# Output weights of a hybrid decoder layer split second half first, in quarters, and the first expert weights issued behind the second branch product

## The chip, the cores and the metric

The kernel runs on one core of one Trainium2 chip. The metric is the device time of one execution in microseconds, and lower is better. Before the change the median of three runs is 793.13 us (791.08 to 793.21).

## The reference, cut to what matters

One decoder layer on a sequence of 512 tokens with a model width of 1024, all in float32. The mixer gives two branch outputs of width 512, one by gated linear attention and one by sparse attention. Each is projected to the model width, gated and added, and the sum goes through the output projection. A mixture of 32 experts follows.

```python
gates = jax.nn.sigmoid(bg.reshape(B, S, N_BRANCHES, D))
mix = gates[:, :, 0] * y_gla + gates[:, :, 1] * y_dsa
out = mix @ w_out[l]
x = x + gate_m * rmsnorm(out, g_post_mix[l])
h = rmsnorm(x, g_pre_ffn[l]) * (1.0 + scale_f) + shift_f
y = hier_moe(h, ...)      # top-1 of 4 groups, top-2 of 8 experts in it, gated MLPs
x = x + gate_f * rmsnorm(y, g_post_ffn[l])
```

## The kernel before, in words

Tokens lie in four tiles of 128 rows (`tt` = 0 to 3), and weights are taken in halves of 512 output columns (`n` = 0, 1). Most projections are done as split products: each float32 operand is written as a high part, rounded to `fp32r`, and a low part, the rest. TensorE then multiplies high by high, high by low and low by high (`split_matmul`, L480 to L482). The high part is a cast on ScalarE (`split_hi`, L1313, semaphore `hi_ready`). The low part is a subtraction on VectorE (`split_lo`, L1794, semaphore `lo_ready`), and it waits for the high part. Both take a whole weight (128x4096 elements) or one quarter of it (128x1024). `split_at` gives each weight its place in the order in which these two semaphores are counted, so whoever waits for a weight also waits for all that stand ahead of it in `split_order`.

The large on-chip `arena` is cut into areas 0 to 3, "H" and "B", and "G" is the tile `gvs`. The two halves of the output weights, `("out", 0)` and `("out", 1)`, live in "H" with their high part in "B", and in "G" with their high part in area 1.

Transfers are issued from SyncE's queue (SP) in a written order. `items` numbers the weights, and `ring_out` counts the products that are done with theirs. Item 18, `("out", 1)`, is loaded once `ring_out` is 15. Item 17, `("out", 0)`, waits for 16, the end of the last input projection, since "H" and "B" hold the split activations until then. Behind item 17, SP issues `first_gate_up(0)`: 2 MB of the first expert's gate and up weights in rows of 1 KB, into area 0. It then waits for `ring_out` 17 (`("proj", 1)` + 1, the end of the second branch product) and issues `first_gate_up(1)` and two down weights of 1 MB each. The next group (`gate_up(1, ...)`, 4 MB) waits for 18, which TensorE signals inside `out_half(2, 1)`, and the one behind it for 19.

TensorE does, in this order, the last input projection, `branches(1, tt)` for four token tiles, `router_bias`, `mix_turn(0)` and `mix_turn(1)` (transposes of the mixed rows), and then the eight `out_half` products. `branches(n, tt)` makes two results of 12 matmuls each in the PSUM banks A0 and A1 by turns. `split_wait(("out", n))` at the head of `out_half` waits for both parts of that weight.

VectorE frees the banks A0 and A1. Per token tile, `mixing(n, tt)` multiplies both results by their gates (L2036) and adds them (L2040). The table `after` says which low parts VectorE works off between two calls of `mixing`. Behind the last `mixing` come `mix_copy(0)`, one more low part and `mix_copy(1)` (L2113). `residual(tt)` (L2078) needs rows of the input `x`, whose transfer ScalarE issues on its own queue (L1585).

On ScalarE, the high parts of both output halves come behind the last `sigmoid`, half 0 first, each as one cast and each behind the wait for its load.

Of the kernel before, what the change touches and what calls it, by code (L numbers as in the profile page):

```python
# [25 lines left out]
D = 1024  # L26
# [55 lines left out]
def layer(nc, x, c, positions, w_ada, b_ada, g_pre_mix, g_post_mix, g_pre_ffn, g_post_ffn, w_in,  # L82
# [17 lines left out]
    with ExitStack() as ctx:  # L100
# [10 lines left out]
        def sem(name):  # L111
            return ctx.enter_context(nc.semaphore(name))
# [123 lines left out]
        ada_spot = (0, 1, "H", "B")  # L236

        split_order = [("in", O_DK), ("in", O_DQ), ("in", O_DV), ("in", O_GQ), ("in", O_GV), ("in", O_GG), ("in", O_BG), ("in", O_BG + D),
                       ("proj", 0), ("in", O_BG + 512), ("in", O_BG + D + 512), ("proj", 1), ("out", 0), ("out", 1)]
        home = {key: ((0, 1), (3, 2))[n % 2] for n, key in enumerate(split_order)}  # L240
        home[("out", 0)], home[("out", 1)] = ("H", "B"), ("G", 1)
        area["G"], area_r["G"] = gvs[:, :], gvs_r[:, :]
# [67 lines left out]
        ring_out = sem("ring_out")  # L310
# [57 lines left out]
        item_at = {it: n for n, it in enumerate(items)}  # L368
# [6 lines left out]
        def ring_wait(eng, it):  # L375
            n = item_at[it]

            extra = sum(1 for m, o in enumerate(items[:n + 1]) if m % 4 == n % 4 and o[0] == "proj")
            eng.wait_ge(ring_in[n % 4], 16 * (n // 4 + 1 + extra))
# [9 lines left out]
        def _(pe):  # L389
# [567 lines left out]
            def other_part(tt):  # L957

                pe.wait_ge(fss_ready, tt + 1)
                for half, (name, _) in enumerate(sum_banks[tt]):  # L960
                    last = nc.tensor.matmul(ps[name][:, :], ident[:, :], yc[:, tt, 0, 512 * half:512 * (half + 1)], start=False, stop=True)
                last.then_inc(sum_full, 1)
# [11 lines left out]
        def _(sp):  # L974
# [59 lines left out]
            def first_gate_up(q):  # L1034
                for n, src in enumerate((w_e_gate, w_e_up)):
                    dst = gu_sets[0][q][:, 2048 * n:2048 * (n + 1)].rearrange("p (k f) -> p k f", k=KD)
                    sp.dma_start(dst, src[0][q].rearrange("(k p) f -> p k f", p=P)).then_inc(we_in[0], 16)
# [10 lines left out]
            def next_down(z, e0, e1_, turn):  # L1048

                sp.wait_ge(bank["A1"].full, moe_base["A1"] + turn)  # L1050
                down(z, 0, e0)
                down(z, 1, e1_)
# [4 lines left out]
            def pair_down(j):  # L1057
                next_down(j % 3, 2 * j, 2 * j + 1, j - 2)

            first_gate_up(0)  # L1060
            sp.wait_ge(ring_out, item_at[("proj", 1)] + 1)
            first_gate_up(1)
            down(0, 0, 0)
            down(0, 1, 1)
# [209 lines left out]
        def _(act):  # L1274
# [34 lines left out]
            def split_hi(key, q=None):  # L1309

                src, _, hi = splits[key]
                part = slice(None) if q is None else slice(1024 * q, 1024 * (q + 1))
                nc.scalar.copy(hi[:, part], src[:, part]).then_inc(hi_ready, 4 if q is None else 1)  # L1313
# [132 lines left out]
            for u in range(NU + 1):  # L1446
                tq, hp = u // PAIRS, u % PAIRS
                n = (tq + 1) * P
# [66 lines left out]
                for tt in range(1, TT):  # L1515
                    sigmoid(1, ab, tt)
            act.wait_ge(ring_out, item_at[("in", O_BG + D + 512)] + 1)
            for n in range(2):
                ring_wait(act, ("out", n))
                split_hi(("out", n))  # L1520

            def out_squares(tt, n):

# [162 lines left out]
            def square(tt):  # L1686

                if tt == 0:
                    act.wait_ge(sum_ready, 1)
                    nc.scalar.activation(scratch2, yc[:, tt, 0, :], ACT.Square, accum_out=st[:, tt:tt + 1]).then_inc(fms_ready, 1)  # L1690
                    return
                act.wait_ge(sum_full, tt + 1)
                for half, (name, _) in enumerate(sum_banks[tt]):
                    n = tt + 20 * half
                    nc.scalar.activation(scratch2[:, 512 * half:512 * (half + 1)], ps[name][:, :], ACT.Square, accum_out=st[:, n:n + 1]).then_inc(fms_ready, 1)
# [19 lines left out]
        def _(dve):  # L1715
# [73 lines left out]
            def split_lo(key, q=None):  # L1789

                src, lo, hi = splits[key]
                part = slice(None) if q is None else slice(1024 * q, 1024 * (q + 1))
                dve.wait_ge(hi_ready, split_at[key] + (4 if q is None else q + 1))
                V.tensor_tensor(lo[:, part], src[:, part], hi[:, part], ALU.subtract).then_inc(lo_ready, 4 if q is None else 1)  # L1794
# [236 lines left out]
            def mixing(n, tt):  # L2031

                for ab in range(2):
                    dve.wait_ge(sig_ready, n * 2 * TT + ab * TT + tt + 1)
                    a, free = filled(dve, ("y", n, tt, ab))
                    step(V.tensor_tensor(sig[:, ab, tt, :], a[:, :], sig[:, ab, tt, :], ALU.mult))  # L2036
                    dve.sem_inc(free, 1)  # L2037
                if n == 0 and tt == 0:
                    filled(dve, ("att", TT * PAIRS - 1), "O")
                V.tensor_tensor(mix[:, tt, n * 512:(n + 1) * 512], sig[:, 0, tt, :], sig[:, 1, tt, :], ALU.add).then_inc(mix_ready, 1)  # L2040
# [3 lines left out]
            split_lo("q")  # L2044
            split_lo(("proj", 0))
            bg0, bg1 = ("in", O_BG + 512), ("in", O_BG + D + 512)
            after = {(0, 1): [(bg0, 0), (bg0, 1)], (0, 2): [(bg0, 2), (bg0, 3)], (0, 3): [(bg1, None)], (1, 0): [(("out", 0), 0), (("out", 0), 1)],
                     (1, 1): [(("out", 0), 2), (("out", 0), 3)], (1, 2): [(("out", 1), 0), (("out", 1), 1), (("out", 1), 2)]}
            for n in range(2):
                for tt in range(TT):  # L2050
                    mixing(n, tt)
                    for key, q in after.get((n, tt), ()):
                        split_lo(key, q)
                if n == 0:
                    split_lo(("proj", 1))
            dve.wait_ge(mix_ready, 2 * TT)

            def shifted(dst, src, k, done, scale, shift):
# [47 lines left out]
            def mix_copy(tt):  # L2106

                if tt >= 2:
                    filled(dve, ("out", tt - 2, 1))
                for half in range(2):  # L2110
                    t, free = filled(dve, ("mix", tt, half))
                    dve.wait_ge(mixT_ready[0], 2 * tt + half + 1)
                    V.tensor_tensor(mixT(tt % 2, 1, 512 * half, 512), t[:, :], mixT(tt % 2, 0, 512 * half, 512), ALU.subtract).then_inc(mixT_ready[1], 1)  # L2113
                    dve.wait_ge(mixT_ready[1], 2 * tt + half + 1)
                    dve.sem_inc(free, 1)
# [39 lines left out]
            dve.sem_inc(free, 1)  # L2155
            step(V.tensor_tensor(w_rt[:, :, :], w_rt[:, :, :], scale_n.unsqueeze(2).broadcast_to([P, KD, GROUPS + NE]), ALU.mult))
            mix_copy(0)
            split_lo(("out", 1), 3)
            mix_copy(1)
            out_scaled(0, 0)  # L2160
            out_scaled(0, 1)
# [180 lines left out]
            def add_last(tt):  # L2342

                dve.wait_ge(fss_ready, tt + 1)
                dve.wait_ge(sum_full, tt + 1)
                for half, (name, _) in enumerate(sum_banks[tt]):
                    y = yc[:, tt, 0, 512 * half:512 * (half + 1)]
                    step(V.tensor_tensor(y, ps[name][:, :], y, ALU.add))
                dve.sem_inc(sum_ready, 1)

            def scaled(tt):

                if tt == 0:
                    step(V.tensor_tensor(yc[:, tt, 1, :], yc[:, tt, 0, :], gfb, ALU.mult))
                else:
                    for half, (name, _) in enumerate(sum_banks[tt]):
                        part = slice(512 * half, 512 * (half + 1))
                        step(V.tensor_tensor(yc[:, tt, 1, part], ps[name][:, :], gfb[:, part], ALU.mult))
# [55 lines left out]
```

## Time and profile before

| | us |
|---|---|
| median of three runs | 793.13 |
| lowest and highest run | 791.08 and 793.21 |
| profiled execution: its span, first to last instruction | 789.2 |
| median less that span, the part outside the first and last instruction, as far as it can be told | 3.9 |
| TensorE busy | 703.0 (89%) |
| VectorE busy | 411.7 (52%) |
| ScalarE busy | 287.7 (36%) |

The trace gives no total of its own for the profiled execution beside the span, so the span and the 3.9 us around it stand for it. Times within the span are counted from its first instruction.

In the page, each digit of a row of 40 is the busy share of one slice of 19.7 us. In a timeline, a row is the start, the duration (the sum, where several instructions follow each other), the engine, the line, the operation, the tiles written and read, their shapes and the count. In square brackets stands how long the engine was idle before it, and what ended that.

### The profile page before, as it was taken

The page shows a single profiled execution, that of the slowest core. Times are in us where ns is not written, and L with a number is a line of the kernel's source. Part 1 is how long each engine was busy: PE and PEld are TensorE (multiplying, and loading weights), DVE is VectorE, ACT ScalarE, POOL GpSimd, SP SyncE. Part 2 cuts the span into 40 slices and gives each one's busy share as a digit, 9 for nine tenths or more (in the row PEclk, how much of TensorE's full clock was granted, in tenths as well). Part 3 has the DMA queues.
Part 4 walks back from the last instruction along what each step waited for, and adds up shares of the span by engine and source line. Part 5 has one row for each costly group of instructions (what it writes and reads, how often), then busy time and mean ns, then how long its engine had stood idle before and what let it go on. Part 6 is the DMA issues. An engine that isn't in the chain of part 4 may idle for free.

```text
span 789.2 us, 9728 instructions
## 1 busy us (share of the span) xinstructions
PE 703.0 (89%) x3451; PEld 447.0 (57%) x3451; DVE 411.7 (52%) x876; ACT 287.7 (36%) x514; POOL 120.9 (15%) x148
## 2 busy tenths in 40 slices
PE   1799989998998999999999899989979978878784
PEld 0347747666776777777787678873423323323221
DVE  2386858998897665654422636572533211112118
ACT  5233255254447768642022315344112211112223
POOL 3064852210002022000000000101121221111100
PEclk9999989999999889999999999999989998989997
DMA  9989730411302030023334472599999999999982
GB/s 337 396 311 364 283 142 1 116 44 64 107 9 99 1 107 1 5 104 107 107 123 161 142 267 79 229 374 391 418 422 418 420 419 419 421 420 413 409 327 108
DMA packets 50300, 179.27 MB, mean 227 GB/s; under 512 B 9624, under 2 KB 13826, under 8 KB 36428
## 3 DMA queue, kind: packets, MB, share of 16 engines
q1 hardware_dynamic: 44308, 166.26, 54.1%
q0 software_dynamic: 4784, 8.19, 2.9%
q10 hardware_dynamic: 1160, 4.20, 1.4%
q8 instruction: 28, 0.46, 0.2%
q14 instruction: 20, 0.16, 0.1%
HBM read 174.13 MB, written 12.59 MB: 237 GB/s over the span
## 4 chain that ended last, share of the span: by engine, by line
PE 48%; SPq 13%; DVE 13%; DMA 8%; ACT 4%; issue 3%; POOL 0%; DVEq 0%; ACTq 0%; POOLq 0%; PEldq 0%
PE psA L480 10%; PE psA L482 10%; PE psA L481 10%; SPq L1032 5%; SPq L1090 4%; SPq L1040 4%; PE psS L884 3%; PE psA L913 3%; DMA arena<-in_w_e_up_dram 2%; PE psG L884 2%; DVE mk_mem L1846 2%; DMA y_dram<-sig_mem,tables 2%; DVE m L1845 2%; PE psO L611 1%; PE psT L598 1%
## 5 line engine op out<-in xcount | busy, mean ns | idle before, releaser
L480 PE MATMUL psA<-arena_r 128*128 128x512 f32 x320 | 130.8, 409 | 3.5 <-DVE arena_r L1794 2.9
L481 PE MATMUL psA<-arena_r 128*128 128x512 f32 x320 | 127.0, 397 | 0.0
L482 PE MATMUL psA<-arena_r 128*128 128x512 f32 x320 | 126.8, 396 | 0.0
L1794 DVE TENSOR_TENSOR arena_r<-arena,arena_r 128x1024 fp32r<-128x1024 f32 (+1 forms) x37 | 60.4, 1654 | 38.4 <-ACT arena_r L1313 37.4
L480 PEld LDWEIGHTS psA<-arena_r 128*128 128x128 f32 x320 | 61.5, 192 | 24.4 <-issue 12.3
L482 PEld LDWEIGHTS psA<-arena_r 128*128 128x128 f32 x320 | 61.5, 192 | 13.5
L481 PEld LDWEIGHTS psA<-arena_r 128*128 128x128 f32 x320 | 61.5, 192 | 12.2 <-issue 0.2
L884 PE MATMUL psG<-arena,kv 128*64 128x512 f32 x208 | 61.2, 642 | 7.6 <-issue 7.6
L884 PE MATMUL psS<-arena,kv 128*64 128x512 f32 x224 | 58.5, 611 | 9.8 <-issue 7.9
L1313 ACT CAST arena_r<-arena 128x1024 fp32r<-128x1024 f32 (+1 forms) x31 | 49.9, 1630 | 20.6 <-DMA arena<-in_w_in_dram 10.2
L913 PE MATMUL psA<-qs_mem,sig_mem 128*64 128x512 f32 x80 | 39.5, 637 | 4.4 <-ACT sig_mem L1637 4.4
L2291 DVE TENSOR_TENSOR sig_mem<-sig_mem,psS 128x256 f32<-128x256 f32 x8 | 4.9, 613 | 72.7 <-ACT sig_mem L1632 72.7
L1239 POOL DMA_INDIRECT y_dram<-sig_mem,tables x16 | 15.9, 994 | 174.6 <-issue 108.5
L480 PE MATMUL psA<-arena_r,qs_mem_r 128*128 128x512 f32 x96 | 38.1, 397 | 4.2 <-DVEq L2037 3.3
L2291 DVE TENSOR_TENSOR sig_mem<-sig_mem,psG 128x256 f32<-128x256 f32 x8 | 4.9, 612 | 70.7 <-ACT sig_mem L1632 70.7
L884 PEld LDWEIGHTS psS<-arena,kv 128*64 128x64 f32 x224 | 20.1, 140 | 37.4 <-issue 36.9
L884 PEld LDWEIGHTS psG<-arena,kv 128*64 128x64 f32 x208 | 19.6, 147 | 33.5 <-issue 32.8
L472 PE MATMUL psA<-arena,kv 128*128 128x512 f32 x64 | 29.2, 619 | 2.3 <-DMA arena<-in_w_in_dram 2.3
L481 PE MATMUL psA<-arena_r,qs_mem_r 128*128 128x512 f32 x80 | 31.1, 389 | 0.0
L1646 ACT COPY sig_mem<-psA 128x512 f32<-128x512 f32 x16 | 9.4, 586 | 55.7 <-PE psA L913 32.2
L1411 ACT ACTIVATE sig_mem<-psA 128x512 f32<-128x512 f32 x16 | 9.6, 598 | 50.8 <-PE psA L482 50.8
L1845 DVE MAX8 m<-mk_mem 128x8 f32<-128x256 f32 (+2 forms) x48 | 26.9, 560 | 2.2
(443 smaller groups left out, 1304.2 us busy)
## 6 DMA issues: line engine op xcount, KB each, us to landing
arena<-in_w_e_gate_dram SPq DMA_DIRECT2D x24, 1024.0 KB, 17.0
arena<-in_w_e_up_dram SPq DMA_DIRECT2D x24, 1024.0 KB, 19.4
arena<-in_w_in_dram SPq DMA_DIRECT2D x11, 2048.0 KB, 8.8
arena<-in_w_e_down_dram SPq DMA_DIRECT2D x12, 1024.0 KB, 18.6
qs_mem<-in_w_e_down_dram SPq DMA_DIRECT2D x10, 1024.0 KB, 23.0
arena<-in_w_ada_dram SPq DMA_DIRECT2D x4, 2048.0 KB, 16.8
qT<-in_w_ada_dram SPq DMA_DIRECT2D x6, 1024.0 KB, 5.4
gvs<-in_w_ada_dram SPq DMA_DIRECT2D x5, 1024.0 KB, 6.3
```

The costliest lines, as they stand in the source:

```text
L472: last = nc.tensor.matmul(a[:, :], hT[:, k, tt * P:(tt + 1) * P], w[:, k, :], start=(k == 0), stop=(k == KD - 1))
L480: nc.tensor.matmul(acc, lhs[0], rhs[0], start=start, stop=False)
L481: nc.tensor.matmul(acc, lhs[0], rhs[1], start=False, stop=False)
L482: return nc.tensor.matmul(acc, lhs[1], rhs[0], start=False, stop=stop)
L884: last = nc.tensor.matmul(ps[g][64 * q:64 * q + 64, :].rearrange("p (g f) -> p g f", g=2), h2g[:, b, k, 64 * q:64 * q + 64], gu, start=(k ...
L913: last = nc.tensor.matmul(ps[name][64 * q:64 * q + 64, :], actT[:, b, kf, 64 * q:64 * q + 64], down_sets[z][q][:, D * kf + 512 * n:D * kf ...
L1032: sp.dma_start(dst, src[bass.ds(e, 1), :, :].rearrange("a p n -> p (a n)")).then_inc(we_in[z], 16)
L1040: sp.dma_start(down_sets[z][q], wed_v[bass.ds(e, 1), :, :].rearrange("a p n -> p (a n)")).then_inc(wd_in[z], 16)
L1090: sp.dma_start(gu_sets[z][q][:, 2048 * n:2048 * (n + 1)][:, part], src[2 * j + q][:, part]).then_inc(we_last[j - (NPAIR - 2)] if half else ...
L1313: nc.scalar.copy(hi[:, part], src[:, part]).then_inc(hi_ready, 4 if q is None else 1)
L1794: V.tensor_tensor(lo[:, part], src[:, part], hi[:, part], ALU.subtract).then_inc(lo_ready, 4 if q is None else 1)
L1845: step(V.max(m8[:, :], work))
```

## The change

The two halves of the output weights change places in `split_order`. ScalarE casts half 1 first and does both in quarters. VectorE's low parts are dealt out anew: one quarter of half 1 comes before the first second-half `mixing`, and none is left between `mix_copy(0)` and `mix_copy(1)`. SP issues `first_gate_up(0)` behind the wait for `ring_out` 17 and no longer ahead of it.

```diff
-                       ("proj", 0), ("in", O_BG + 512), ("in", O_BG + D + 512), ("proj", 1), ("out", 0), ("out", 1)]
+                       ("proj", 0), ("in", O_BG + 512), ("in", O_BG + D + 512), ("proj", 1), ("out", 1), ("out", 0)]
...
+            sp.wait_ge(ring_out, item_at[("proj", 1)] + 1)
             first_gate_up(0)
-            sp.wait_ge(ring_out, item_at[("proj", 1)] + 1)
             first_gate_up(1)
...
             act.wait_ge(ring_out, item_at[("in", O_BG + D + 512)] + 1)
-            for n in range(2):
+            for n in (1, 0):
                 ring_wait(act, ("out", n))
-                split_hi(("out", n))
+                for q in range(4):
+                    split_hi(("out", n), q)
...
-            after = {(0, 1): [(bg0, 0), (bg0, 1)], (0, 2): [(bg0, 2), (bg0, 3)], (0, 3): [(bg1, None)], (1, 0): [(("out", 0), 0), (("out", 0), 1)],
-                     (1, 1): [(("out", 0), 2), (("out", 0), 3)], (1, 2): [(("out", 1), 0), (("out", 1), 1), (("out", 1), 2)]}
+            after = {(0, 1): [(bg0, 0), (bg0, 1)], (0, 2): [(bg0, 2), (bg0, 3)], (0, 3): [(bg1, None)], (1, 0): [(("out", 1), 1), (("out", 1), 2)],
+                     (1, 1): [(("out", 1), 3), (("out", 0), 0), (("out", 0), 1)], (1, 2): [(("out", 0), 2), (("out", 0), 3)]}
...
                 if n == 0:
                     split_lo(("proj", 1))
+                    split_lo(("out", 1), 0)
...
             mix_copy(0)
-            split_lo(("out", 1), 3)
             mix_copy(1)
```

## Rows read from the trace of the kernel before

**Rows 1.** The page: TensorE's total, DMA share and GB/s of 40 slices

```profile
PE 703.0 (89%) x3451; PEld 447.0 (57%) x3451; DVE 411.7 (52%) x876; ACT 287.7 (36%) x514; POOL 120.9 (15%) x148
...
DMA  9989730411302030023334472599999999999982
GB/s 337 396 311 364 283 142 1 116 44 64 107 9 99 1 107 1 5 104 107 107 123 161 142 267 79 229 374 391 418 422 418 420 419 419 421 420 413 409 327 108
```

**Rows 2.** The chain of waits, 395 to 540 us: start, us, what

```profile
428.73 7.84 DMA arena<-in_w_out_dram
436.67 3.64 ACT arena_r L1313
...
443.50 0.47 PE psA L480
...
461.02 0.43 PE psA L480
...
472.65 0.87 PE psS L726 x8
```

**Rows 3.** Timeline of ScalarE around the casts of the output weights

```profile
428.71 0.60 ACT L1411 ACTIVATE sig_mem<-psA 128x512 f32<-128x512 f32 x1 [4.84 <-PE psA L482]
436.67 3.63 ACT L1313 CAST arena_r<-arena 128x4096 fp32r<-128x4096 f32 x1 [7.37 <-DMA arena<-in_w_out_dram]
```

**Rows 4.** All casts of line 1313: ns least, median, most

```profile
L1313 ACT CAST arena_r<-arena x31: 1031/1050/3635, 42.1 to 436.7; 128x1024 fp32r<-128x1024 f32 x24, 128x4096 fp32r<-128x4096 f32 x7
```

**Rows 5.** Timeline of TensorE, 425 to 470 us

```profile
439.76 0.39 PE L482 MATMUL psA<-arena_r,qT_r 128*128 128x512 f32 x1
443.50 0.47 PE L480 MATMUL psA<-arena_r,qs_mem_r 128*128 128x512 f32 x1 [3.35 <-DVEq L2037]
...
449.06 0.39 PE L480 MATMUL psA<-arena_r,qs_mem_r 128*128 128x512 f32 x1
...
454.28 0.39 PE L482 MATMUL psA<-arena_r,qT_r 128*128 128x512 f32 x1
454.97 1.95 PE L745 MATMUL psG<-w_rt,gla_mem 128*128 128x36 f32 x16 [0.30 <-PE psA L482]
...
459.08 1.94 PE L726 MATMUL psS<-ident,kv 128*128 128x128 f32 x8 [1.27 <-DVEq L2115]
```

**Rows 6.** Timeline of VectorE, 430 to 476 us

```profile
432.10 0.69 DVE L2036 TENSOR_TENSOR sig_mem<-psA,sig_mem 128x512 f32<-128x512 f32 x1 [9.75 <-PE psA L482]
434.82 0.69 DVE L2036 TENSOR_TENSOR sig_mem<-psA,sig_mem 128x512 f32<-128x512 f32 x1 [2.03 <-PE psA L482]
435.66 0.69 DVE L2040 TENSOR_TENSOR kv<-sig_mem 128x512 f32<-128x512 f32 x1
440.33 2.36 DVE L1794 TENSOR_TENSOR arena_r<-arena,arena_r 128x1024 fp32r<-128x1024 f32 x2 [3.98 <-ACT arena_r L1313]
442.61 0.68 DVE L2036 TENSOR_TENSOR sig_mem<-psA,sig_mem 128x512 f32<-128x512 f32 x1
...
450.78 3.49 DVE L1794 TENSOR_TENSOR gvs_r<-gvs,arena_r 128x1024 fp32r<-128x1024 f32 x3
454.19 0.68 DVE L2036 TENSOR_TENSOR sig_mem<-psA,sig_mem 128x512 f32<-128x512 f32 x1
...
475.70 1.42 DVE L2078 SCALAR_TENSOR_TENSOR gqk<-gqk,st,qs_mem 128x512 f32<-128x512 f32 x2
```

**Rows 7.** Timeline of SP's queue: transfers of output and expert weights

```profile
407.37 0.51 SPq L1000 DMA_DIRECT2D gvs<-in_w_out_dram  x1
...
454.79 0.37 SPq L1037 DMA_DIRECT2D arena<-in_w_e_gate_dram  x1
...
501.91 0.33 SPq L1032 DMA_DIRECT2D arena<-in_w_e_gate_dram  x1
```

**Rows 8.** Windows: us, PE, PEld, DVE, ACT, POOL busy (count), PEclk, DMA share, GB/s

```profile
440.20:443.50 3.30, 0.00 (x1) 0.03 (x1) 2.96 (x3) 3.30 (x2) 0.00 (x0) 1.00 0.55 173
454.80:470.50 15.70, 14.27 (x72) 12.22 (x73) 6.70 (x11) 2.93 (x6) 0.00 (x0) 0.89 0.91 333
459.00:462.00 3.00, 2.92 (x11) 2.62 (x12) 2.54 (x4) 1.17 (x2) 0.00 (x0) 0.50 1.10 363
472.00:498.00 26.00, 26.00 (x149) 22.37 (x148) 14.59 (x43) 14.35 (x25) 3.71 (x2) 1.00 0.17 62
506.00:736.00 230.00, 203.80 (x1016) 88.93 (x1014) 70.36 (x202) 55.13 (x125) 30.46 (x30) 0.96 1.01 412
```

**Rows 9.** Transfer queues from 466 to 467 us: packets, MB, share of 16 engines

```profile
q1 hardware_dynamic: 34, 0.28, 66.8%
q10 hardware_dynamic: 33, 0.14, 33.7%
```

**Rows 10.** Transfers of `x` rows issued at line 1585, and one at line 1537

```profile
L1585 ACTq DMA_DIRECT2D qs_mem<-in_x_dram x2: 388/414/440, 461.1 to 461.5; - x2
...
DMA to landing us min/median/max: 8.2/9.3/10.5
...
qs_mem<-in_x_dram ACTq DMA_DIRECT2D x1, 512.0 KB, 3.1
```

## The prediction

> **What bounds the kernel now.** I read the page first. TensorE is busy for 89% of the span, but the last third tells another story: from slice 27 to 38 the DMA row is at 9 and the rate near 420 GB/s [rows 1]. A window confirms it: from 506 to 736 us the share is 1.01 at 412 GB/s, while TensorE has 26 us idle in these 230 [rows 8]. The expert stage is a stream of weights that runs back to back once it is released. The release is SP's issue at 501.91 us, which waits for a product inside the output projection [rows 7]. So what counts is how early that point comes.
>
> The chain of waits leads back from there. From 461 us to the release it is TensorE at work with no gap. Ahead of it stands one detour: the load of half 0 of the output weights (428.73, 7.84 us), its cast (436.67, 3.64 us), and only at 443.50 a matmul again [rows 2]. The timelines show how a load for a later product stops this one. ScalarE is free after its sigmoid at 429.3 us, but its first cast waits 7.37 us for that load [rows 3]. VectorE is done with the first `mixing` at 436.3 us and stands at the low part of half 0 for 3.98 us. After two low parts it gets to the next gate multiplication at 442.61 [rows 6]. TensorE holds both PSUM banks full meanwhile: its last matmul starts at 439.76, the next at 443.50, 3.35 us idle [rows 5].
>
> **The casts and low parts: the wait goes, a small one comes.** Matmuls here start every 0.227 us (449.06 to 454.28 us is 23 steps, 5.22 us) [rows 5]. Without a wait the matmul of 443.50 would start at 439.76 + 0.23 = 439.99.
>
> Half 1 was issued at 407.37 us [rows 7], over 20 us before `ring_out` reached 16. Its first quarter is cast at 429.3 to 430.35 (1.05 us, the median of that form) and the fourth is done by 433.5 [rows 3, 4]. Its first low part (1.18 us, half of 2.36) ends at 431.6. It stands ahead of the `mixing` that started at 432.10 after 9.75 us idle [rows 6], so it costs nothing; its cover is 0.5 us, and a cast later by more than that would push the mixing one for one. The quarters of half 0 follow the landing, 436.6 us, and end by 440.9. Four quarters cost 4 x 1.05 = 4.2 us against 3.63 for the whole [rows 4]; the next work of ScalarE is over 10 us later, so 0.6 us is hidden.
>
> VectorE, by the distances of its rows [rows 6]: two low parts of half 1 from 436.3, then the gate multiplication at 438.5, which ends at 439.2. A bank comes free 0.89 us after such a start (442.61 to 443.50 [rows 5, 6]), at 439.4, so TensorE goes on at 439.99. The second result is complete at 440.15; multiplication at 440.26, addition at 441.1. Now come three low parts, where before there were two. Three of them and the next multiplication are 3.41 us apart (450.78 to 454.19 [rows 6]): 441.7 + 3.41 = 445.1. The bank is free at 446.0. TensorE wants it at 439.99 + 24 x 0.227 = 445.43. That is what is late next, **0.57 us**, a wait that was not there.
>
> The matmul of 449.06 us thus starts at 446.0, 3.06 us sooner. A restart costs about 0.1 us (the first step is 0.30 and not 0.227), in both kernels, once at another place. The last matmul of the branch products moves from 454.28 to about 451.3, **3.0 us** sooner. The two low parts left (447.5 to 449.9) fall under TensorE's work. All eight are there by 449.9, so the wait of `out_half` for both halves costs nothing: that product starts near 461.0 - 3.0 = 458.0 [rows 2]. The cover is 8 us.
>
> The low part taken out between `mix_copy(0)` and `mix_copy(1)` (1.2 us) stands behind the bank release that TensorE waits for at 459.08 [rows 5], and ahead of rows needed a product later. I count it at 0; its bounds are 0 and 0.2 us.
>
> **The moved transfers.** SP issued the first 2 MB right behind half 0. Now they stand behind `ring_out` 17, 454.79 - 3.0 = 451.8 us, with the other 4 MB. Queued behind them on SP is the group that waits for 18, near 498.9, and nothing else. Moved are six transfers, 6.29 MB, and 1.05 MB of `x` rows from ScalarE: 7.34 MB. At the 333 GB/s of the same stretch [rows 8] they end at 451.8 + 22.0 = 473.8 us. From there to the release the chip moves little now (share 0.17 from 472 to 498 [rows 8]), so the cost to the stream is 0. Without that idle stretch 2.1 MB at 412 GB/s would cost 5.1 us. The experts first need the weights after 530 us.
>
> The `x` rows are the near miss. They were issued at 461.1, landed 8.2 and 10.5 us later [rows 10] and were first needed at 475.70 [rows 6]. Now they are issued near 458.1 and needed at 472.7, with some 2.1 MB more ahead. If the transfers share the engines as before, the first tile lands at 466.3: cost 0. If it has to stand behind the extra 2.1 MB as well (5.8 us at 363 GB/s), it lands at 472.1: still 0, by 0.6 us. What speaks for sharing: from 466 to 467 us ScalarE's queue (q10) moved 33 packets and SP's (q1) 34 [rows 9]. The Trainium skill (DMA: Bandwidth & Descriptors, section on queues, rings and completion order) says that each engine goes round between the queues packet by packet; by that rule, the trace agrees, the first landing applies.
>
> **Sum.** 3.51 us of wait gone, less 0.57 of new wait: 3.0 rounded. The expert stream, its releases and the tail keep their distances. The profiled execution has a span of 789.2 and gets 786.2; the median lies 3.9 us over that span, and the same 3.9 gives 790.1. As the runs spread over 2.1 us, this stall may have been longer or shorter in others; it ends with the landing of one load.
>
> **Rivals.**
> A. The clock stretch goes. The clock granted to TensorE is 1.00 through the idle 440.2 to 443.5, but 0.50 (1.2 GHz) from 459 to 462 [rows 8]. There eight transposes take 1.94 us [rows 5] and 0.87 us later on, and three to four matmul steps 0.43 instead of 0.23 [rows 2]: 1.07 + 0.7 = 1.8 us. With other timing ahead it may be spared: 788.3. The Trainium skill (TensorE: Matmul & The Clock Gate, part 1) says that the chip's measure runs free of the program, so an equal gap can fall either way.
> B. The reverse: one more such stretch, beside the new small wait or ahead of the output products: 790.1 + 1.8 = 791.9. For it: the gap at 459 was only 1.27 us. Against: the long gap at 440 did not do it.
> C. It does nothing: the expert stage takes its pace from elsewhere, or half 0 lands so late that VectorE still waits. 793.1. Against: the engine row is full from 506 us, and half 0 is cast 5 us before it is wanted (437.7 against 442.9).
> D. Slower: the `x` rows are served only after all SP transfers. 6.29 MB at 333 GB/s end at 470.7, and a tile alone takes 3.1 us [rows 10]: 473.8. `residual(0)` then comes 1.1 us late, and TensorE's transposes, which follow it, by some 0.6: 790.7. It decides against the kernel only if the rows of 1 KB run slower. At 280 GB/s the tile lands at 477.4, and the time is 794.3; the change loses from 476.2 on, about 295 GB/s. Against: 363 GB/s from 459 to 462 us, in these very rows [rows 8].
>
> **How the numbers follow.** Forecast 0.60 (own range 789.0 to 791.4: the new wait between 0 and 1.5 us, and a stall of another length), A 0.10, B 0.11, C 0.08, D 0.11, of it 0.04 near 790.7 and 0.07 at 793 and above. The range 788.0 to 793.0 takes in A, B and the mild end of D, and leaves out most of C and the rest of D, about 0.15 to 0.2. No change is within 0.3%, 2.4 us, about what a measurement of this kernel can tell. The forecast clears it by 0.6 us only, so a fifth of its chance falls within. Faster: 0.48 of the forecast and 0.10 of A, 0.58. Within: 0.12 of the forecast, B, C and the mild D, 0.35. Slower: 0.07.
>
> **What would show it.** Casts of half 1 from 429 us in quarters; no idle TensorE at 440, and about 0.6 us near 445.5; last branch matmul at 451.3; SP's group of six at 451.8; the release at 498.9; all later marks 3 us sooner. A first `x` tile landing after 472.7, or clock 0.50 elsewhere between 440 and 500, would make the number wrong, and so would a stream whose end does not follow its release.

## The result and the profile after

| | before | changed |
|---|---|---|
| median of 13 runs, us | 791.41 (788.33 to 796.73) | 785.11 (783.77 to 790.76) |
| ratio, changed to before | | 0.9942, 95% interval 0.9922 to 0.9963 |
| span of the profiled execution, us | 789.2 | 789.0 |

The change makes the kernel 4.6 us faster by the ratio (2.9 to 6.2 us), and 6.3 us by the medians. The forecast was 3.0 us faster, 790.1 us in a range of 788.0 to 793.0, so the direction was right, and the time lies below the range. The interval of this ratio takes in the forecast's 3.0 us, so it does not show by itself that the gain is larger. In the experiments below two single executions took 2402.74 us (the kernel before) and 3903.55 us (both gaps filled), which the ratios leave out.

The two profiled executions hide this. The changed one took 790.76 us, the slowest of its 13 runs, and its span equals that of before. The profile's page shows the same work in it:

```profile
PE 704.7 (89%) x3451; PEld 448.5 (57%) x3451; DVE 411.9 (52%) x876; ACT 289.0 (37%) x520; POOL 120.6 (15%) x148
...
DMA  9989740402303030033324293699999999999972
```

So the stage has to be read by itself. On ScalarE, half 1 is cast in quarters right behind the last sigmoid, and half 0 from its landing on (timeline of ScalarE, changed kernel):

```profile
431.48 3.91 ACT L1313 CAST arena_r<-gvs 128x1024 fp32r<-128x1024 f32 x4 [0.17 <-ACT sig_mem L1411]
438.72 3.91 ACT L1313 CAST arena_r<-arena 128x1024 fp32r<-128x1024 f32 x4 [3.34 <-DMA arena<-in_w_out_dram]
```

VectorE, same kernel. The 3.98 us ahead of the low parts of half 0 [rows 6] are gone, and the first low part is done 0.38 us before the first mixing can start:

```profile
432.56 1.23 DVE L1795 TENSOR_TENSOR gvs_r<-gvs,arena_r 128x1024 fp32r<-128x1024 f32 x1 [8.05 <-ACT arena_r L1313]
434.17 0.69 DVE L2037 TENSOR_TENSOR sig_mem<-psA,sig_mem 128x512 f32<-128x512 f32 x1 [0.38 <-PE psA L482]
...
444.91 2.35 DVE L1795 TENSOR_TENSOR arena_r<-arena,arena_r 128x1024 fp32r<-128x1024 f32 x2
447.18 0.69 DVE L2037 TENSOR_TENSOR sig_mem<-psA,sig_mem 128x512 f32<-128x512 f32 x1
```

TensorE, same kernel: its rows with an idle time, and the one ahead of the new wait. In place of 3.35 us idle [rows 5] there is one wait of 0.41 us, behind the three low parts in a row. Counted as the prediction counts, from where the next matmul would have started (447.27 + 0.23), it is 0.57 us:

```profile
431.05 0.47 PE L480 MATMUL psA<-arena_r,qs_mem_r 128*128 128x512 f32 x1 [0.44 <-PE psA L482]
...
447.27 0.39 PE L482 MATMUL psA<-arena_r,qT_r 128*128 128x512 f32 x1
448.07 0.47 PE L480 MATMUL psA<-arena_r,qs_mem_r 128*128 128x512 f32 x1 [0.41 <-DVEq L2038]
...
454.05 1.95 PE L745 MATMUL psG<-w_rt,gla_mem 128*128 128x36 f32 x16 [0.30 <-PE psA L482]
...
458.17 1.94 PE L726 MATMUL psS<-ident,kv 128*128 128x128 f32 x8 [1.27 <-DVEq L2117]
```

From the first matmul of the second branch product to the router bias it takes 454.05 - 431.05 = 23.00 us. Before it took 454.97 - 429.02 = 25.95 us; the first matmul of the kernel before is

```profile
429.02 0.47 PE L480 MATMUL psA<-arena_r,qs_mem_r 128*128 128x512 f32 x1 [0.41 <-PE psA L482]
```

That is 2.95 us less. But this execution came to the stage 2.03 us later, and it had 0.86 us more behind the first expert product.

SP's queue and the windows of the changed kernel (us, PE, PEld, DVE, ACT, POOL busy, PEclk, DMA share, GB/s):

```profile
453.87 0.37 SPq L1037 DMA_DIRECT2D arena<-in_w_e_gate_dram  x1
...
500.86 0.33 SPq L1032 DMA_DIRECT2D arena<-in_w_e_gate_dram  x1
```

```profile
453.87:473.00 19.13, 17.68 (x91) 15.11 (x92) 5.96 (x12) 3.72 (x9) 0.00 (x0) 0.91 0.99 340
457.00:462.00 5.00, 3.83 (x15) 3.31 (x16) 2.77 (x4) 1.81 (x4) 0.00 (x0) 0.66 1.10 359
...
505.00:735.00 230.00, 203.17 (x1011) 89.19 (x1011) 70.30 (x202) 55.31 (x125) 30.32 (x30) 0.96 1.01 412
```

The six transfers move through an otherwise idle stretch, and the expert stream keeps its share of 1.01 and 412 GB/s [rows 8]. The clock at the first transposes fell in this execution too. The `x` rows, moved earlier with the rest, landed faster than before [rows 10]:

```profile
L1586 ACTq DMA_DIRECT2D qs_mem<-in_x_dram x2: 388/414/439, 460.2 to 460.6; - x2
...
DMA to landing us min/median/max: 7.1/7.8/8.4
```

### The profile page after: what moved, and what is told of

Its sections match the earlier page's. It is cut to its first block, busy times and chain, and to the rows that moved or that the text cites. A ratio compares the mean times of both kernels' runs of the same rounds, so it can differ in the third digit from the quotient of the medians.

```text
span 789.0 us, 9733 instructions
## 1 busy us (share of the span) xinstructions
PE 704.7 (89%) x3451; PEld 448.5 (57%) x3451; DVE 411.9 (52%) x876; ACT 289.0 (37%) x520; POOL 120.6 (15%) x148
## 4 chain that ended last, share of the span: by engine, by line
PE 56%; DVE 13%; DMA 7%; SPq 5%; issue 5%; ACT 3%; POOL 0%; DVEq 0%; ACTq 0%; POOLq 0%
PE psA L480 11%; PE psA L482 10%; PE psA L481 10%; PE psS L884 5%; PE psA L913 5%; SPq L1090 4%; PE psG L884 4%; DMA arena<-in_w_e_up_dram 2%; DVE mk_mem L1847 2%; DMA y_dram<-sig_mem,tables 2%; DVE m L1846 2%; PE psO L611 1%; PE psT L598 1%; PE psS L588 1%; DMA xn_dram<-sig_mem 1%
```

## The experiments

Two questions: which edit gives the 2.95 us, and where the rest of the 4.6 us comes from. The expectations name three theories: the wait alone counts (1), the wait and falls of TensorE's clock count (2), the moved transfers matter (3). "The stage" is the stretch from the first matmul of the second branch product to the router bias, and a "fall" is a stretch in which the granted clock is 0.50. All ratios are to the kernel before, run beside each kernel.

**The two kernels again, and the change in two parts.** The first kernel is the one before and the second the changed one, both unedited.

> The kernel before, unchanged, under a name of its own, to see how far two sets of executions of one kernel lie apart on this chip and what granted clock each has. Theory 1 (the stall alone): the branch-product stretch from the first matmul of the second branch product to the router bias is 25.9 us as in the trace before, and the time is equal to before within 0.2%. Theory 2 (stall plus clock): the idle 3.35 us at 440 us also lets TensorE's clock fall to half in some executions, so the executions fall into groups 2 to 5 us apart, and the slower group has the lower mean clock. Theory 3 (the moved transfers matter): says nothing on this one.

> The changed kernel, unchanged, beside the others of this job. Theory 1: 3.0 us (0.38%) under before, the rest of the 4.6 us (ratio 0.9942) being chance in when the executions were taken. Theory 2: 4 to 6 us under before, with a mean clock higher by 0.003 to 0.006. The branch-product stretch is 23.0 us in its trace under either.

The SP edit alone:

```diff
-            first_gate_up(0)
             sp.wait_ge(ring_out, item_at[("proj", 1)] + 1)
+            first_gate_up(0)
             first_gate_up(1)
```

> Only the SP edit: the first expert's 2 MB behind the wait for the second branch product, nothing else changed. Theory 1 and 2: the stall at 440 us stays 3.3 us, give or take 0.5, the time is that of before within 0.2%. Theory 3: the load of half 0 lands sooner without 2 MB behind it (under 7 us instead of 7.84), the stall shrinks by as much, and the time falls by 1 to 2 us.

All but the SP edit:

```diff
-            sp.wait_ge(ring_out, item_at[("proj", 1)] + 1)
             first_gate_up(0)
+            sp.wait_ge(ring_out, item_at[("proj", 1)] + 1)
             first_gate_up(1)
```

> All of the change but the SP edit: half 1 first, quarters, low parts dealt out anew, the first expert's 2 MB issued early as before. Theory 1: the stall is gone, the time is that of the changed kernel within 0.1%, 3 us under before. Theory 2: the same, 4 to 6 us under before. Theory 3: between before and the changed kernel, at least 1 us over the changed one.

| | median, us | ratio, 95% interval |
|---|---|---|
| before again | 789.20 | 0.9979 (0.9954 to 1.0004) |
| changed again | 784.70 | 0.9926 (0.9887 to 0.9964) |
| SP edit alone | 789.56 | 0.9985 (0.9959 to 1.0012) |
| all but the SP edit | 785.29 | 0.9940 (0.9913 to 0.9968) |

The unedited kernel lies 0.2% from itself, so differences of that size are not told apart here. Its twelve executions (786.35 to 792.21 us) do not part into the groups that theory 2 asked for. The SP edit does nothing that can be seen, and the split order with its quarters does all that can be seen. The load of half 0 is not helped by having no 2 MB behind it: with the SP edit alone it lands in 7.8 us (the least of the two output loads; 7.84 before [rows 2]), and ScalarE's wait for it (7.4 us) and VectorE's behind that (3.97 us) are as before (output weights' transfers, and timeline of VectorE).

```profile
  ACT arena_r L1313: 7.4, 1
...
DMA to landing us min/median/max: 7.8/10.1/12.4
```

```profile
441.72 2.36 DVE L1794 TENSOR_TENSOR arena_r<-arena,arena_r 128x1024 fp32r<-128x1024 f32 x2 [3.97 <-ACT arena_r L1313]
```

Theory 3 falls by this wait; the time alone would not rule out its 1 to 2 us. The trace of the kernel before, taken again, shows what that of the prediction did not. Its matmuls behind the wait start every 0.43 us and not every 0.23 us, at a granted clock of 0.57 in the window (timeline of TensorE and a window):

```profile
440.73 0.70 PE L480 MATMUL psA<-arena_r,qs_mem_r 128*128 128x512 f32 x1 [3.48 <-DVEq L2037]
441.23 0.63 PE L481 MATMUL psA<-arena_r,qs_mem_r 128*128 128x512 f32 x1
441.65 0.63 PE L482 MATMUL psA<-arena_r,gqk_r 128*128 128x512 f32 x1
```

```profile
440.50:444.50 4.00, 3.77 (x10) 2.99 (x11) 3.64 (x5) 0.53 (x1) 0.00 (x0) 0.57 0.00 0
```

The stage took 27.68 us in this execution instead of 25.95: 1.7 us for one fall. And in the changed kernel's second trace the clock stays full at the first transposes, where it fell in the first one:

```profile
451.00:460.00 9.00, 7.55 (x42) 6.19 (x42) 3.42 (x6) 2.25 (x4) 0.00 (x0) 1.00 1.07 356
```

**The wait in another size.** The kernel before, with the casts in quarters only:

```diff
                 ring_wait(act, ("out", n))
-                split_hi(("out", n))
+                for q in range(4):
+                    split_hi(("out", n), q)
```

> The kernel before with one edit: the high parts of both halves cast in quarters, half 0 still first. The first low part can start about 1.0 us after the load and not 3.6 us after it, so TensorE's wait at 440 us should shrink from 3.5 to about 1.0 us. Theory 1 (the wait alone): 2.4 to 2.6 us under before. Theory 2 (wait plus clock): 3.5 to 4.5 us under before, as a short wait no longer lets the clock fall, and no stretch at 0.50 between 438 and 446 us in the trace. A third possibility, that only a load out of the way helps: no gain.

788.12 us, ratio 0.9968 (0.9944 to 0.9991). The wait is 0.87 us:

```profile
436.98 0.47 PE L480 MATMUL psA<-arena_r,qs_mem_r 128*128 128x512 f32 x1 [0.87 <-DVEq L2038]
```

The stage took 23.50 us, 2.45 less than before, and the ratio gives 2.5 us. That was theory 1's number. Theory 2 was right that no fall comes near 440. Its 3.5 to 4.5 us did not appear, though the interval (0.7 to 4.4 us) does not rule them out, and the trace has a fall at 514 to 518 us instead. Most of the stage's gain was to be had with these two lines.

**Work in the gaps.** `filler` writes products nobody reads into a free bank. The kernel before with the wait filled:

```diff
             for tt in range(TT):
+                if tt == 2:
+                    filler("S1", 12)      # 12 matmuls of 512 columns
                 branches(1, tt)
```

> The kernel before with 12 extra matmuls (2.7 us) into an unused bank at the place of the wait at 440 us, so that TensorE is at work in nearly all of the wait, which itself stays. The extra products are thrown away. Theory 1: the same time as before within 0.1%. Theory 2: 0.8 to 1.8 us under before, the share of executions in which the clock fell there times its price of about 1.7 us. If the filler delays the product behind it, up to 0.3 us more.

788.25 us, ratio 0.9975 (0.9951 to 0.9999): 2.0 us, just above theory 2's 0.8 to 1.8. There was no fall at 440, while the stage (26.36 us) was not shorter than in the trace of the prediction, which had no fall there either. The interval nearly reaches 1, and the kernel against itself gave 0.9979, so this alone shows little.

The changed kernel with the second gap filled:

```diff
             mix_turn(0)
+            split_wait(("out", 1))
+            filler("O", 5)
             mix_turn(1)
```

> The changed kernel with 5 extra matmuls (1.1 us) into an unused bank between the two first transposes of mixed rows, where TensorE idles 1.27 us. Their results are thrown away. Theory 2 and rival A of the prediction (the half-clock stretch at 457 to 462 us hangs on this gap): the stretch goes in all executions, 1 us gained on the mean over the changed kernel, router bias to first output product 5.35 us and not 5.71. Theory 1: the same time as the changed kernel within 0.1%, or 0.2 us more.

783.73 us, ratio 0.9922 (0.9899 to 0.9945), with the clock full:

```profile
451.00:460.00 9.00, 8.71 (x46) 6.95 (x45) 3.42 (x6) 2.25 (x4) 0.00 (x0) 1.00 1.08 360
```

The full clock stood there without the filler in three of four traces of this product order, all three of executions that came early to the stage, as this one did (see the table below). So the gain over the changed kernel (0.2% by ratio) is not shown.

Both gaps filled in the kernel before, by the two edits together, with half 0 as the second filler's operand:

> The kernel before with extra matmuls in both gaps: 12 in the wait at 440 us and 5 between the two first transposes of mixed rows. Their results are thrown away. Theory 1: the time of before within 0.1%. Theory 2: 2 to 3 us under before; what then stays to the changed kernel with the second gap filled alike is the bare wait, 2.9 us.

789.34 us (788.73 without the one long execution), ratio 0.9990 (0.9970 to 1.0010): a miss for theory 2. The trace has no fall at 440 or at the transposes, but one at 528 to 532 us, and the stretch to the first expert product is 110.6 us, longer than in the trace of the prediction (109.8). With both gaps filled a fall still came, only later.

**The wait put back.** The changed kernel, with TensorE waiting at the old place for something VectorE finishes about 3 us later:

```diff
             for tt in range(TT):
+                if tt == 2:
+                    pe.wait_ge(lo_ready, split_at[("out", 1)] + 4)
                 branches(1, tt)
```

> The changed kernel, with an idle wait put back at the old place: TensorE waits ahead of the third token tile of the second branch product for the last low part of half 1, about 3.0 us idle, while the 0.4 us wait one tile later falls away. Casts, low parts and transfers stay as changed. Theory 1 (the wait alone counts): 2.6 us over the changed kernel. Theory 2 (wait plus clock): 3.5 to 4.5 us over it, so within 1 us of before, and the granted clock falls to 0.50 behind the wait or at the first transposes in more of the executions.

The same with `filler("S1", 11)` ahead of the wait:

> The kernel of the run ahead with 11 extra matmuls (2.5 us) into an unused bank inside the wait. Their results are thrown away. The wait's end is the same, TensorE is only not idle in it. Theory 1: the time of the run ahead within 0.1%. Theory 2: 1 to 1.7 us under it, and 2.6 us over the changed kernel.

Idle: 789.73 us, ratio 0.9985 (0.9967 to 1.0002), the kernel before again. Filled: 787.41 us, ratio 0.9968 (0.9946 to 0.9989). Windows of the two at the wait:

```profile
441.00:446.00 5.00, 4.96 (x15) 3.96 (x16) 2.50 (x3) 0.00 (x0) 0.00 (x0) 0.66 0.00 0
```

```profile
441.00:446.00 5.00, 4.67 (x21) 3.55 (x20) 4.48 (x5) 0.16 (x1) 0.00 (x0) 1.00 0.00 0
```

The idle wait costs 3.4 us over the changed kernel by the ratios (0.9985 against 0.9942), the filled one 2.1 us, with 2.4 us more in the stage. The order is that of theory 2, with sizes just under its 3.5 to 4.5 and 2.6. But the intervals of the two overlap, and theory 1's 2.6 us for both lies within both, so the times do not decide.

**The delay as work, in two sizes.** The changed kernel with 13, then 7, extra matmuls at that place, with no wait:

```diff
+                if tt == 2:
+                    filler("S1", 13)      # and 7
```

> The changed kernel with 13 extra matmuls (2.95 us) into an unused bank ahead of the third token tile of the second branch product: the old delay back, but as work and with no idle at all. Their results are thrown away. Theory 2a (the idle wait lets the clock fall): 2.6 us over the changed kernel (the 0.4 us wait one tile later falls away), with no fall at 440 us. Theory 2b (the delay itself moves the later gaps to where the clock falls): 3.5 to 4.5 us over it, with a fall between 455 and 530 us.

> The same with 7 extra matmuls (1.59 us). Theory 2a: 1.2 us over the changed kernel. Theory 2b: anything from 1.2 to 3 us over it, by where the gaps then come to lie; a fall between 455 and 530 us in the trace if it is over 2.

13: 785.98 us, ratio 0.9949 (0.9930 to 0.9968), the stage 2.26 us longer, no fall from 435 to 530 us. 7: 786.48 us, ratio 0.9959 (0.9935 to 0.9983), the stage 1.07 us longer, a fall at 520 to 524 us. The larger delay does not bring the loss back (0.6 us by ratio, even under theory 2a's 2.6), so theory 2b does not hold as put. Its interval is some 1.5 us wide on each side, as is that of the changed kernel, so theory 2a's 2.6 is not ruled out. The trace of the smaller one has a fall without any whole idle wait ahead of it, so theory 2a is not all either. That of the larger one is of an execution that came late to the stage, that of the smaller one of an early one, so the two are not quite alike.

**One more trace of each, and the version from it.**

> The kernel before, one more trace. Both theories below need the count of executions in which the granted clock falls between 435 and 545 us. If a fall belongs to the kernel with the wait, there is at least one here, as in the two traces of it so far, and the stretch from the first matmul of the second branch product to the first expert product takes 109.8 us or more.

> The changed kernel, one more trace. If the falls went with the wait, there is none between 435 and 545 us and the stretch takes 105.6 us, as in one of the two traces of it so far; the other had one fall and 106.7 us.

The trace of before had falls at 439 to 444 and 456 to 461 us, the changed one none from 435 to 530. The small new wait is taken out by one low part moved on:

```diff
-(1, 1): [(("out", 1), 3), (("out", 0), 0), (("out", 0), 1)], (1, 2): [(("out", 0), 2), (("out", 0), 3)]}
+(1, 1): [(("out", 1), 3), (("out", 0), 0)], (1, 2): [(("out", 0), 1), (("out", 0), 2), (("out", 0), 3)]}
```

> The changed kernel with one low part moved on: two and not three behind the second mixing, three behind the third. The wait at 448 us (0.4 us, predicted as 0.57) should be gone, first matmul to router bias 22.6 us and not 23.0. Theory 1 and 2 alike: 0.4 us under the changed kernel, which the time alone can hardly tell; if the third mixing then holds up the transposes, no gain or 0.3 us lost.

783.22 us, ratio 0.9918 (0.9893 to 0.9943). The stage took 22.35 us, 0.65 less than changed: the 0.57 us of the wait and its restart. With the filler between the transposes as well:

> The best version so far: the changed kernel with two and not three low parts behind the second mixing, and 5 extra matmuls between the first two transposes. Their results are thrown away. Both theories: 0.4 us under the kernel with the extra matmuls alone, some 7 us under before (ratio 0.991), if the two edits add up; the same as either if the first one brought nothing.

782.76 us over six executions, ratio 0.9906 (0.9880 to 0.9932), the fastest kernel here, ahead of both. Its interval overlaps that of the one ahead of it and that of the changed kernel.

## Where the 4.6 us come from

The table sets marks side by side in all traces, in us, from the timelines of TensorE and SP. The marks are the first matmul of the second branch product (its time stands in the first column), the router bias (L745), the first output product, and SP's first issue behind the first expert product. The last column says where the granted clock was under 1 from 435 to 530 us.

| kernel | first matmul at | first matmul to bias | bias to output product | first matmul to expert product | clock fell near |
|---|---|---|---|---|---|
| before, of the prediction | 429.0 | 25.95 | 5.71 | 109.8 | 459 |
| before again | 426.1 | 27.68 | 5.71 | 111.6 | 440, 457 |
| before, one more | 425.3 | 27.77 | 5.71 | 111.6 | 439, 456 |
| SP edit alone | 430.4 | 26.04 | 5.71 | 109.9 | 460 |
| changed | 431.1 | 23.00 | 5.71 | 106.7 | 457 |
| changed again | 426.3 | 22.96 | 5.35 | 105.6 | none |
| changed, one more | 427.2 | 23.17 | 5.34 | 105.9 | none |
| all but the SP edit | 426.1 | 22.96 | 5.35 | 105.6 | none |
| quarters only | 424.9 | 23.50 | 5.34 | 107.7 | 514 |
| before, wait filled | 430.7 | 26.36 | 5.71 | 110.1 | 460 |
| before, both filled | 429.9 | 26.29 | 5.34 | 110.6 | 528 |
| changed, idle wait back | 427.1 | 27.04 | 5.34 | 111.3 | 441, 520 |
| changed, wait filled | 429.5 | 25.44 | 5.35 | 109.7 | 521 |
| changed, 13 extra | 429.7 | 25.26 | 5.34 | 107.9 | none |
| changed, 7 extra | 424.6 | 24.07 | 5.34 | 108.4 | 520 |
| changed, transposes filled | 426.0 | 22.97 | 5.34 | 105.7 | none |
| changed, low part moved | 426.6 | 22.35 | 5.34 | 105.0 | none |
| both of these | 425.2 | 22.32 | 5.35 | 105.0 | none |

The first four have TensorE's order of before, the next four that of the change. Their means over the whole stretch are 110.7 and 106.0 us, a difference of 4.7 us, and the ratio says 4.6. It has three parts:
- The wait: 2.95 us, in every pair without a fall at it.
- A fall at the wait: 1.7 us, in two of the four traces of before and none of the changed. Of all traces it comes in three of the five with the whole wait idle, and in none of the 13 others. That gives 0.9 us on the mean.
- A fall at the first transposes: 0.36 us to the output product, and 0.8 us within it and its followers up to the release (40.4 against 41.2 us), 1.15 us in all. It comes in four of four before and one of four changed, which gives 0.9 us on the mean.

A fall near 514 to 528 us, in five of the other traces, takes 1.5 to 1.6 us between the release and the first expert product (38.5 against 36.9 us).

That 4.7 meets 4.6 so closely is luck, as each mean rests on four traces and the ratio's interval is 2.9 to 6.2 us. That the gain is over 3.0 us is better founded: the 33 executions of the changed order in the first two measurements have a mean of 785.9 us, the 68 of the order of before, SP edit alone counted in, 790.4, which is 4.6 us, by their scatter 3.6 to 5.6 (an estimate; it pools two measurements).

**The falls go with the arrival.** The first column parts the traces into two groups that the list above mixes. In seven the first matmul comes late, at 429.0 to 431.1 us, in eleven early, at 424.6 to 427.2. That is settled ahead of anything that differs between these kernels: from 268 to 284 us the granted clock was 0.68 or less in each of the seven, and 1.00 in each of the eleven (windows of before, then of before again):

```profile
268.00:284.00 16.00, 15.64 (x83) 11.64 (x84) 6.98 (x21) 7.90 (x20) 4.03 (x5) 0.68 0.00 2
```

```profile
268.00:284.00 16.00, 15.25 (x116) 11.54 (x116) 10.30 (x28) 10.12 (x22) 4.04 (x5) 1.00 0.01 2
```

Five traces have the whole wait idle. The clock fell behind it in the three early ones (before again, before one more, idle wait back) and in neither of the two late ones (before, SP edit alone). The length of the idle time does not sort them: 2.83, 3.48 and 3.51 us were followed by a fall, 3.33 and 3.35 us were not. At the transposes the order of before has a fall in both groups, and the changed order only in the one late trace of its four (two late traces with a delay put into it had none there). So over the stretch to the first expert product the change takes 3.1 us off a late execution (109.8 and 109.9 to 106.7) and 5.9 us off an early one (111.6 twice to 105.6, 105.9 and 105.6). The 4.6 us is a mix of the two, and how often each comes was not measured. These two prices rest on few traces, one changed one for the late group.

## Why the prediction was wrong, step by step

**Casts and low parts: right.** No wait was left at the third tile. The new one at the fourth came as 0.41 us idle, which by the prediction's own count is its 0.57 us. The stage lost 2.95 us for a forecast of 3.0. The 0.5 us of cover for the first low part was 0.38 us.

**The moved transfers: right.** The group was issued 22.8 us behind the first matmul, as worked out (451.8 against 429.0). The `x` rows landed 7.1 us after their issue, so rival D is out, and the SP edit alone changes nothing that can be seen. Rival C is out as well: the expert stream follows its release, 249.5 to 251.3 us from the first expert product to the end in all traces but one (253.5).

**The sum: this is the step that failed.** "The expert stream, its releases and the tail keep their distances", and before that 3.51 less 0.57, took the clock of one execution as a fixed part of the kernel and put what the clock would change at nothing. The rows showed a long idle wait without a fall, and the argument read that as a property of the wait. In executions that come early to the stage the same wait costs 1.7 us more, and the fall at the transposes, kept in the sum on both sides, is gone with the change in them. On the mean of the traces these two terms make some 1.7 us. Rival A had the last one, at 1.8 us for a measured 1.15, and gave it a chance of 0.10, where three of four traces show it. It counted the eight transposes at 0.87 us without a fall; they take 1.47 us from first start to last end, with 0.19 us of waiting for VectorE among them (changed again):

```profile
453.36 0.63 PE L726 MATMUL psS<-ident,kv 128*128 128x128 f32 x4 [1.26 <-DVEq L2117]
454.17 0.66 PE L726 MATMUL psS<-ident,kv 128*128 128x128 f32 x4 [0.19 <-DVEq L2117]
```

Rival B's argument "the long gap at 440 did not do it" rested on one trace, of a late execution, and the next trace refutes it.

**The step to the median** was off by 1.7 us as well. It put 3.9 us around the span, where every profiled execution since shows about 1.8 us between span and time (790.76 against 789.0). By that the profiled execution of before was the one of 791.08 us: near the later median of 791.41 over 13 executions, and 2 us under the 793.13 of the first three.

Either of the two alone would have left 788.4 us, inside the range. Together they give 786.7, and by the ratio 786.8. The median of 785.11 lies 1.7 us lower still. Eight of the 13 changed executions took 783.8 to 786.0 us at a mean granted clock of 0.963 to 0.968, and four took 788.4 to 790.8 at 0.959 to 0.961, the profiled late one among them (787.17 lies between). The median stands in the lower heap and says nothing of the upper one. That the upper heap is the late arrival fits the traces and is not shown for executions without one.

**What stays open** is what makes an execution early or late, and how that decides the later falls. All traces with the fall at the wait are early and have the whole wait idle. But a fall near 520 us came with a gap filled, with the wait shortened to 0.87 us and with a delay of 1.1 us without idle, in early and in late executions, and a delay of 2.3 us as work brought none in a late one. One trace of each such kernel is too few to tell the length of the delay from chance.

## What to carry to other kernels

Ahead of a product that two engines prepare operands for, order the preparation by when its data lands and in pieces no longer than the slack of the results that share the engine. Here quartering the casts alone removed 2.45 of 2.95 us. Price an idle wait of TensorE by its length plus the chance of a clock fall times its price, and read that chance from several traces. Sort these traces first by when they reach the stage, and compare early ones with early ones: here the arrival told where the clock fell, and the length of the wait did not. Where the profile gives a span, find what lies around it from one run that has both, before adding it to a median.

## What the hardware showed unexpectedly

The granted clock after the same idle wait is not fixed: 3.35 us idle left it at 1.00 in the trace of the prediction, 3.48 us idle was followed by matmuls at 0.43 us a step in the next, and 2.83 us idle by a fall too (0.66 from 441 to 446 us in the kernel with the wait put back). What went with it was the granted clock from 268 to 284 us, over 150 us earlier. Two transfers issued on ScalarE's queue at 460.2 us did not stand behind the 6.3 MB that SP's queue issued from 453.9 to 466.5 us: 512 KB each landed in 7.1 and 8.4 us, against 8.2 and 10.5 us before. They did share with them, as one alone took 3.1 us [rows 10].
